# Expert 0's input rows: a product with a 0/1 slot matrix on TensorE in place of a gather and a turn

## The reference

```
logits = (xt @ w_router) + router_bias
probs  = softmax(logits)                    # 16 experts in 4 groups
g_idx  = the group with the largest sum of its two best probs
top_w, top_i = top_k(probs inside that group, 2);  top_w /= sum(top_w)
for e in range(16):
    h = silu(xt @ w_gate[e]) * (xt @ w_up[e])          # 1024 -> 512
    y = y + gates[:, e:e+1] * (h @ w_down[e])          # 512 -> 1024
```

## Time and profile before

| | |
|---|---|
| median of 3 runs | 703.26 us (702.64 to 706.01) |
| profiled execution | 706.77 us, of which the span of the trace is 704.9 us |
| mean granted TensorE clock | 0.974 |
| PE / DVE / ACT / POOL busy | 671.2 / 503.6 / 344.3 / 134.9 us |
| DMA | 162.56 MB, mean 231 GB/s |

### The profile page before, as it was taken

The page is one execution under the profiler, slowest core; times in us unless marked ns, Lnnn a source line. Parts: engine busy times, 40 slices in busy tenths (PEclk is TensorE's granted clock), DMA queues, the critical chain, the costliest instruction groups (busy, mean ns, idle before and its releaser), DMA issues. The chain is left out here.

```text
span 704.9 us, 9687 instructions
## 1 busy us (share of the span) xinstructions
PE 671.2 (95%) x3863; PEld 563.5 (80%) x3863; DVE 503.6 (71%) x576; ACT 344.3 (49%) x338; POOL 134.9 (19%) x81
## 2 busy tenths in 40 slices
PE   6999999988999999999978999999999999999796
PEld 5999899988997887567856888888888888888531
DVE  4326346799666284757495999999999999999526
ACT  4438412222236231011415777777777777777302
POOL 0000414433031210400021011111111111100064
PEclk9999999999999999999799999999999999999997
DMA  9951111211613005069227999999999999993163
GB/s 288 382 185 61 60 60 61 70 53 58 202 43 109 23 16 191 0 209 419 97 84 304 364 377 416 410 402 419 413 402 415 404 410 410 411 405 148 60 248 133
DMA packets 48689, 162.56 MB, mean 231 GB/s; under 512 B 4294, under 2 KB 23450, under 8 KB 36364
## 3 DMA queue, kind: packets, MB, share of 16 engines
q1 hardware_dynamic: 41756, 136.62, 51.0%
q0 software_dynamic: 6896, 25.43, 9.2%
HBM read 142.61 MB, written 19.44 MB: 230 GB/s over the span
## 5 line engine op out<-in xcount | busy, mean ns | idle before, releaser
L1309 DVE TENSOR_TENSOR RA<-FA,RA 128x2048 fp32r<-128x2048 f32 x93 | 212.8, 2289 | 28.6 <-ACT RA L854 28.0
L854 ACT ACTIVATE RA<-FA 128x2048 fp32r<-128x2048 f32 x93 | 178.9, 1924 | 45.0 <-PE bank L1753 28.9
L1753 PE MATMUL bank<-RA 128*128 128x512 f32 x768 | 186.1, 398 | 2.3 <-DVE RA L1314 2.1
L1753 PEld LDWEIGHTS bank<-RA 128*128 128x128 f32 x768 | 142.3, 190 | 34.0 <-DVE RA L1314 3.0
L1491 PE MATMUL bank<-RA 128*128 128x272 f32 x432 | 110.4, 292 | 0.0
L1492 PE MATMUL bank<-RA 128*128 128x272 f32 x432 | 109.7, 290 | 0.0
L1765 PE MATMUL bank<-RA 128*128 128x512 f32 x384 | 89.9, 390 | 1.4 <-DVE RA L1319 1.4
L1765 PEld LDWEIGHTS bank<-RA 128*128 128x128 f32 x384 | 72.0, 188 | 16.5 <-DVE RA L1319 1.6
L1491 PEld LDWEIGHTS bank<-RA 128*128 128x128 f32 x432 | 82.6, 191 | 0.0
L1492 PEld LDWEIGHTS bank<-RA 128*128 128x128 f32 x432 | 82.4, 191 | 0.0
L978 DVE TENSOR_TENSOR RA<-FA,RA 128x2048 fp32r<-128x2048 f32 (+1 forms) x18 | 48.6, 2700 | 28.6 <-ACT RA L712 28.3
(11 more groups left out here) (227 smaller groups left out, 764.9 us busy)
## 6 DMA issues: line engine op xcount, KB each, us to landing
FA<-w_up SPq DMA_DIRECT2D x32, 1024.0 KB, 7.3
FA<-w_gate SPq DMA_DIRECT2D x32, 1024.0 KB, 6.9
FA<-w_down SPq DMA_DIRECT2D x32, 1024.0 KB, 7.7
FA<-w_in SPq DMA_DIRECT2D x13, 1024.0 KB, 5.0
y_by_slot<-FA POOLq DMA_DIRECT2D x16, 512.0 KB, 7.7
y_by_slot<-FA POOLq DMA_DIRECT2D x1, 4096.0 KB, 17.1
FA<-w_out SPq DMA_DIRECT2D x4, 1024.0 KB, 5.1
FA<-x_prompt SPq DMA_DIRECT2D x8, 256.0 KB, 5.8
```

Of the source, the lines that this page charges most:

```text
L854: nc.scalar.activation(split[split_slot(bi, j)][0], raw[place], ACT.Copy).then_inc(m_hi, 1)
L1309: tt_(sl[1], raw[place], f(sl[0]), ALU.subtract).then_inc(m_lo, 1)
L1753: last = mm(out[:, :], xgT[par][x_][:, kt, :], w[w_][:, t, :], start=(kt == 0 and i == 0), stop=(kt == KT - 1 and i == 2))
```

## The change

Expert 0's turned rows are no longer gathered and transposed. DVE builds for each token tile a 128 x 128 matrix in f32 (`one_hot[1]`): a 1 at (token, r) where one of the token's two slots is r, for r below 128, which are the slots of expert 0. PE multiplies x1 (stationary, every fourth column, straight from `xr`) with it over the 5 token tiles, 40 matmuls, and the result stands in banks 0 and 1 as the turned block did. `keep_clock(28)` and `x_turn(0, 0)` go. POOL's first gather is that of expert 1, and expert 2's follows it with no wait. The cast of `ids` moves behind DVE's three `first_lo`, and SP's load of raw buffer 7 waits for it instead of for the first turn.

```
@@ one tile more, one semaphore more
+        one_hot = [fa(AT0 + NTT * D - 2 * H * T + i * NTT * P, NTT * P).rearrange("p (t r) -> p t r", t=NTT) for i in range(2)]
+        s_m0 = sem("rows_of_expert0")
@@ SP
             moe_loads(2, 2, (0,))
-            sp.wait_ge(m_t, 1)
+            sp.wait_ge(s_ids, 1)
             load(7, source(3, 1, 0))
@@ POOL
             pool.wait_ge(s_ids, 1)
-            gather(0, 0)
             gather(1, 1)
-            pool.wait_ge(m_t, 1)
             gather(2, 0)
@@ DVE, behind slot_f
+            rows0 = const[:, C_IO:C_IO + P]
+            link(tt_(one_hot[0], rows0.unsqueeze(1).broadcast_to([P, NTT, P]),
+                     slot_f[:, 0:NTT].unsqueeze(2).broadcast_to([P, NTT, P]), ALU.is_equal))
+            for tt in range(NTT):
+                stt(one_hot[1][:, tt, :], rows0, slot_f[:, NTT + tt:NTT + tt + 1], one_hot[0][:, tt, :],
+                    ALU.is_equal, ALU.add).then_inc(s_m0, 1)
+
             n_sl = 2 * NTT
             link(nc.vector.tensor_copy(slot_i[:, :], slot_f))
...
                     row[:, sl].unsqueeze(2).broadcast_to([P, NTT, P]), ALU.is_equal).then_inc(s_hot, 1)
-            dve.wait_ge(s_tab, 1)
-            nc.vector.tensor_copy(ids[:, :], bank[5][:, 0:NBLK]).then_inc(s_ids, 1)
...
             first_lo(0)
             first_lo(1)
             first_lo(2)
+            dve.wait_ge(s_tab, 1)
+            nc.vector.tensor_copy(ids[:, :], bank[5][:, 0:NBLK]).then_inc(s_ids, 1)
             overflow_table()
             x_lo(0, 0)
@@ PE
             keep_clock(12)
+            pe.wait_ge(s_m0, NTT)
+            pe.wait_ge(s_x1, NTT)
+            for c in range(2):
+                for t in range(4):
+                    for tt in range(NTT):
+                        rows = P if tt < 4 else NS
+                        last = mm(bank[c][:, t * P:(t + 1) * P], xr[0:rows, tt, c * 512 + t:(c + 1) * 512:4],
+                                  one_hot[1][0:rows, tt, :], start=(tt == 0), stop=(tt == NTT - 1))
+            last.then_inc(m_t, 1)
             for n in range(2):
                 pe.wait_ge(s_hot, n + 1)
...
-                pe.wait_ge(m_xg[par], 8 * (bi - par) + 16)
-                if not (isinstance(bi, int) and bi == 0):
-                    pe.wait_ge(m_tl, 2 * bi)
+                pe.wait_ge(m_xg[par], 8 * (bi - par) + 16 * par)
+                pe.wait_ge(m_tl, 2 * bi)
...
-            keep_clock(28)
-            x_turn(0, 0)
             step(0, 0)
```

## The result

The changed kernel takes 720.24 us (median of 6 runs, 716.8 to 723.73) against 702.95 us for the kernel before (6 runs, 701.96 to 706.71): ratio 1.0226, with a 95% interval of 1.0196 to 1.0256. It is slower by 17.3 us between the medians and by about 16 by the ratio, where 705.0 was forecast with a range of 702 to 708 and 79% for no change that a measurement can tell.

The account below looks back on a forecast made before the run. PE was taken to set the loop's pace, so a later start moves the end equally. +1.5 us (start) and +0.3 (clock) made +1.8, from 703.26 to 705.0 us; range 702 to 708, 79% within 0.5%.

Parts of the forecast that it names:

- the rate of the 40 products: On PE ahead of the token table: 80 records at 0.118 us each, 9.4 us in all.
- The upper bound, 0.14 a record: On PE: a strided stationary side might cost 0.14 us a record, making the products 11.2 us instead of 9.4.
- the forecast of the start: Start of step(0, 0), the first gate product: 1.5 us later, at 376.15 instead of 374.63.
- The price of being late: At DVE's wait for the token table: each microsecond PE is late delays step(0, 0) equally; 0.1 us was added.
- Rival 1: PE late with the token table through a fallen clock or dearer strided loads: 706.8 to 708.5 us, 16% chance.
- DVE's part: Six added DVE operations ahead of slot_i: 1.85 us, between 1.7 and 2.2.
- The two even chains at `x_lo`: Before x_lo(0, 0), the gather's chain and DVE's own order end within 0.2 us, DVE's being later.
- The term of 0.3 for the clock: First gate products on PE: half clock again for 2 to 5 us after 5.7 us idle, costing 0.3 us more.
- I expect the 40 products at full clock: On PE: the products run at clock 1.00, as an earlier stretch of 74 plain f32 records did.
- Gathers and loads: Expert 1's gather lands at 379.3 to 382.4, needed at 383.6; PE waits for none of SP's moved loads.
- The rival of the late gather: Expert 1's gather, sharing DMA engines with weight loads, lands at 386.5 and holds PE 2.9 us: 707.9 us, 5% chance.
- The loop's period: In the expert loop: the period stays unchanged, so a shift of the start moves the end by as much.

Follow-up runs that it names:

- experiment 2: Changed kernel with the fifth token tile multiplied with all 128 rows instead of 32; 717.0 us against 701.3 for the kernel before.
- experiment 3: Changed kernel with 22 instead of 12 keep_clock matmuls ahead of the 40 products; 717.7 us against 701.3 for the kernel before.
- experiment 1: Changed kernel with x1's columns read contiguously instead of every fourth, expert 0's output not the reference's; 716.8 us against 701.3 for the kernel before.
- experiment 5: Changed kernel with contiguous columns, all tiles at 128 rows, expert 0's four gate and up chunks loaded in matching row order; 706.85 us against 704.59 before, ratio 1.0029.
- experiment 8: Kernel before the change with x_lo(0, 0) moved ahead of overflow_table(), nothing else; 702.65 us against 704.59, ratio 0.9985.
- experiment 7: experiment 5 with ACT and DVE working on bank 0 while PE fills bank 1, DVE reordered, 22 keep_clock matmuls; 707.2 us against 704.59 before, ratio 1.0034.
- experiment 6: experiment 5 with x_lo(0, 0) moved ahead of overflow_table(); 704.23 us against 704.59 for the kernel before, ratio 1.0005.
- experiment 10: Changed kernel with all token tiles at 128 rows and x1 read at every second column, output not the reference's; 708.4 us against 703.24 before.
- experiment 9: experiment 7 with the token table's matmuls between the products' halves and ids cast right behind first_lo(0); 700.43 us against 703.24 before, ratio 0.9951.

## Why the prediction was wrong

**What failed is one term, the rate of the 40 products.** The step was: "The stationary side here is read at every fourth column; the turn of expert 0's rows reads so too, and 8 records took 1.23 cold-started and 1.12 warm, 0.12 a record: no dearer. So 80 x 0.118 = 9.4". The row was right and the transfer from it wrong. A transpose shows one record for each operation and runs at 0.12 with the stride; an f32 product shows two, and each took 0.233 with the stride (in the changed kernel, and at full clock in experiments 2 and 3). Neither could be read from the other. The upper bound, 0.14 a record, came from the same wrong neighbour, so the range was too narrow as well. The rows of before held no f32 product with a strided stationary side; that should have been a reason for a wide bound.

**A second thing wasn't counted at all**: eight times PE goes from 128 rows to 32 and back. It costs 4.6 us (experiment 2), of which 3.5 are the idle 0.22 us of PEld, 16 times.

The two make up the loss: 23.5 us (changed kernel), 18.9 without the changes of row count, 9.2 with contiguous columns too. 4.6 + 9.7 = 14.3, of the 16.0 by which the start moved. The other 1.7 are what is left of the change without them; the forecast of the start was 1.5 and experiment 5 measured 1.6. The shares hang on the order: taken first, contiguous columns brought only 2.4 (experiment 1, with the clock at 0.50 to the end), and the row counts behind them 11.8. Each cure is worth most with the other.

**The price of being late was named and was right.** "If PE is late by x, then the cast, the overflow table, `x_lo` and `step(0, 0)` are late by x" is what happened, with x at 14 instead of 0.1. Rival 1 had this place and two of the three mechanisms (the clock, a strided load), with 16% and a price of 1.7 to 3.5 us; the price was too small by a factor of four or more, and the changes of row count were not in it.

**DVE's part**: 1.85 us forecast for the six operations, with 2.2 as a bound; from 356.86 to 359.04 it is 2.18, since the five small ones stand 0.26 apart and not 0.20. The overflow table takes 4.4 instead of 4.2.

**The two even chains at `x_lo`** were read rightly: experiment 8 gained the 0.2 us. So the gather wasn't what PE waited for in the end, and its removal alone could gain nothing.

**The clock**: the first gate product ran at 0.53 of full speed and took 5.5 us (389.45 to 394.91, when ACT is released) instead of 4.7, the bad end of what the prediction allowed. The term of 0.3 for the clock came out as 0.8 over the first 24 matmuls (8.13 against 7.35). But "I expect the 40 products at full clock" was wrong. The stretch it rested on the earlier trace rows has other products: its loads are contiguous, and most of its tiles are 128 x 32.

**Gathers and loads** were hidden as forecast in the changed kernel. The rival of the late gather, given 5%, became real only when the start was early (experiment 7).

**The loop's period** didn't change: from one turn to the next there are 17.9 us, and the shift was carried to the end. "PE's one listed wait of a matmul" is one of two: the same view has a second of 0.8 us, which changes nothing in the reading.

## What to carry to other kernels

Take the rate of a matmul only from a row that has the same kind of operation, the same type and the same read pattern of the stationary side; a transpose is no measure of an f32 product. Keep the rows of consecutive matmuls equal, by padding if that is harmless, and don't judge such a cure by itself: here the two together gave 14.3 us, and alone 2.4 and 4.6. And when a transfer is taken off a path, look for the next one that becomes due: here the gain came only once the next gather was issued earlier.

## What the runs showed of the hardware

Loads of a 128 x 128 f32 stationary tile for a product stand 0.112 us apart with contiguous columns, 0.118 with every second, and 0.233 with every fourth. The last figure is the same at the half clock and at the full one. The Trainium skill, "SBUF — State Buffer", section "Door 1: The DMA port swizzle", says that reads are at full bandwidth if at least two in a row fall into one line of 16 bytes. With every second f32 column two do, with every fourth one does, and the three figures agree with that. It also puts the free stride at 4 for f32, which doesn't agree with the 0.233. The transposes fit neither: they read with the same stride and start 0.12 apart, and why stays open.

Going between a 128-row and a 32-row f32 tile left the weight load idle for 0.22 us each time at half clock, in the changed kernel and in experiment 1 alike, and for 0.19 at full clock (experiment 1). With such changes in it, a PE that was shown busy without a gap ran at 1.2 GHz for 22 us; without them the clock came back to 2.4 GHz within the products (experiments 2, 6 and 10) or never fell (experiments 5, 7 and 9). The changes are not enough by themselves: the kernel before goes between 32 and 128 rows every 2.9 us in the stretch from 254.5 to 264 us, with tiles of other widths, and its clock there is 1.00. PE in that stretch:

```profile
257.88 0.40 PE L1619 MATMUL bank<-FA 32*32 32x128 f32 x2
258.21 1.94 PE L1621 MATMUL bank<-FA 128*32 128x128 f32 x16
260.17 0.66 PE L1613 MATMUL bank<-FA 128*128 128x128 f32 x4
```

What makes the difference stays open.
